# A decoder block on one core: forget gates computed in the first value projection, a third gate tile ahead of the recurrent projections, the causal mask added by VectorE, norm steps reordered

## The reference, cut to what matters

```python
xr = causal_dwconv(xr, w_rnn_conv[l], b_rnn_conv[l])
hr = rg_lru(xr, w_lru_a[l], b_lru_a[l], w_lru_i[l], b_lru_i[l], lru_lambda[l])
y_rnn = gelu(gr) * hr
log_f = log_sigmoid(fl + b_fgate[l])
F = cumsum(log_f, axis=1)                                    # over the tokens, by head
s = q k^T / sqrt(128) + F[q] - F[k], masked to k <= q        # by head, in blocks of 128 tokens
y_attn = softmax(s) v
merged = g_r * (y_rnn @ w_proj_rnn) + g_a * (y_attn @ w_proj_attn)
x = x + gate1 * (merged @ w_out)
h = modulate(rmsnorm(x, g_norm2), shift2, scale2)            # then the ConvFFN, and a last modulated norm
```

## Time and profile before

| | |
|---|---|
| median of 3 runs (lowest, highest) | 983.5 us (982.2, 983.51) |
| the profiled execution: time, span | 983.65 us, 981.9 us |
| TensorE (PE) busy | 968.5 us, 99% |
| VectorE (DVE) busy | 635.5 us, 65% |
| ScalarE (ACT) busy | 415.8 us, 42% |
| mean granted TensorE clock | 0.993 |
| waits of TensorE on the trace | 3.1, 1.2, 1.0, 0.7 and 0.5 us, one each |
| DMA | 129.37 MB, mean 132 GB/s |

### The profile page before, as it was taken

How to read it: one execution, slowest core, us unless ns; L and a number is a source line. 1 busy time by engine, 2 the same in 40 slices (tenths; PEclk the granted TensorE clock), 3 DMA queues, 4 the chain that set the end, 5 groups by cost and what they waited for, 6 DMA issues and landing times.

```text
span 981.9 us, 12554 instructions
## 1 busy us (share of the span) xinstructions
PE 968.5 (99%) x4739; PEld 816.5 (83%) x4739; DVE 635.5 (65%) x856; ACT 415.8 (42%) x548; POOL 2.2 (0%) x12
## 2 busy tenths in 40 slices
PE   8999999999999999999999999999999999999997
PEld 8878887788888888989888889888888888888875
DVE  3789998522668797853758555777674344754665
ACT  6479777322426354352623373322232222422331
POOL 0000000000000000000000000000000000000000
PEclk9899999999999999999999999999999999999999
DMA  9743311334674435432217505666532332233201
GB/s 326 249 139 102 102 43 49 96 96 131 210 232 151 153 116 181 129 107 86 86 44 259 192 21 172 196 200 202 180 118 86 105 109 85 86 106 136 100 20 67
DMA packets 105775, 129.37 MB, mean 132 GB/s; under 512 B 4636, under 2 KB 81156, under 8 KB 105612
## 3 DMA queue, kind: packets, MB, share of 16 engines
q1 hardware_dynamic: 105192, 126.75, 39.5%
q10 hardware_dynamic: 548, 2.14, 0.6%
HBM read 126.77 MB, written 2.11 MB: 131 GB/s over the span
## 4 chain that ended last, share of the span: by engine, by line
PE 94%; DVE 3%; DMA 1%; SPq 1%; issue 0%; ACT 0%; DVEq 0%; ACTq 0%
PE ps L1667 30%; PE ps L1669 30%; PE ps L1668 30%; DMA ada_first<-in_w_ada 1%; PE ps L1900 1%; PE ps L1711 1%; DVE wsplit_x L1570 0%; DVE wraw_x L1566 0%; PE ps L1726 0%; PE ps L1719 0%; PE ps L1701 0%; PE ps L1700 0%; PE ps L2017 0%; DVE act_s L1583 0%; SPq L447 0%
## 5 line engine op out<-in xcount | busy, mean ns | idle before, releaser
L1667 PE MATMUL ps<-h,wsplit 128*128 128x512 f32 (+1 forms) x816 | 312.7, 383 | 1.2 <-DVE h L1539 1.2
L1669 PE MATMUL ps<-h,wsplit 128*128 128x512 f32 (+1 forms) x816 | 310.9, 381 | 0.0
L1668 PE MATMUL ps<-h,wsplit 128*128 128x512 f32 (+1 forms) x816 | 310.8, 381 | 0.0
L988 DVE TENSOR_TENSOR wsplit<-wraw,wsplit 128x2048 fp32r<-128x2048 f32 (+2 forms) x79 | 167.0, 2114 | 101.6 <-ACT wsplit L596 64.1
L1667 PEld LDWEIGHTS ps<-h,wsplit 128*128 128x128 f32 x816 | 153.6, 188 | 29.9 <-issue 1.4
L1669 PEld LDWEIGHTS ps<-h,wsplit 128*128 128x128 f32 x816 | 153.4, 188 | 29.5
L1668 PEld LDWEIGHTS ps<-h,wsplit 128*128 128x128 f32 x816 | 153.5, 188 | 28.8
L596 ACT ACTIVATE wsplit<-wraw 128x2048 fp32r<-128x2048 f32 (+2 forms) x69 | 120.9, 1752 | 105.2 <-PE ps L1669 104.8
L1596 DVE SCALAR_TENSOR_TENSOR cv<-ps,vec,cv 128x511 f32<-128x511 f32 (+1 forms) x48 | 35.9, 748 | 55.7 <-ACT cv L945 52.6
L1041 DVE SCALAR_TENSOR_TENSOR ada_acc<-ada_raw,small,ada_acc 128x512 f32<-128x512 f32 x84 | 63.1, 751 | 2.7
L1667 PE MATMUL ps<-wsplit,act_s 128*128 128x512 f32 x160 | 62.3, 390 | 0.7 <-DVE act_s L1583 0.7
(11 more groups left out here) (248 smaller groups left out, 1415.7 us busy)
## 6 DMA issues: line engine op xcount, KB each, us to landing
wraw<-in_w_ffn_up SPq DMA_DIRECT2D x24, 1024.0 KB, 5.1
wraw<-in_w_in SPq DMA_DIRECT2D x23, 1024.0 KB, 5.3
ada_raw<-in_w_ada SPq DMA_DIRECT2D x16, 1024.0 KB, 6.7
wraw<-in_w_ffn_down SPq DMA_DIRECT2D x10, 1024.0 KB, 4.9
ada_first<-in_w_ada SPq DMA_DIRECT2D x8, 1024.0 KB, 12.1
ada_raw<-in_w_ada_final SPq DMA_DIRECT2D x8, 1024.0 KB, 5.1
wraw<-in_w_in SPq DMA_DIRECT2D x12, 512.0 KB, 3.8
wraw<-in_w_proj_rnn SPq DMA_DIRECT2D x8, 640.0 KB, 4.4
```

Of the source, the lines that this page charges most:

```text
L988: ve.tensor_tensor(wsplit[:, s, LO, 0:n], wraw[:, s, 0:n], wsplit[:, s, HI, 0:n].bitcast(F), ALU.subtract).then_inc(w_lo, 1)
L1667: te.matmul(dst, lhs(LO), rhs(HI), start=start, stop=False)
L1668: te.matmul(dst, lhs(HI), rhs(LO), start=False, stop=False)
L1669: return te.matmul(dst, lhs(HI), rhs(HI), start=False, stop=stop)
```

## The change

- The forget-gate product and its small weight buffer go. The first value projection (`v_first`) is made ahead of q and k, with weights `vw` of 256 + 8 columns, into four banks; its last eight columns are the forget gates, tokens on partitions. Their log-sigmoid is computed there, four transposes bring it to 8 partitions for the scan, and the transposes for `nFq` move between the two k tiles. The chunk order becomes v, q, k; the q tiles of pair 0 use banks 5 and 6. SP stores and reloads `nF` inside the first `load_step`.
- The third gate tile is made where the forget-gate product was, in bank 3. The loop of pairs has five rounds instead of six, and projections 13, 14 and 15 follow each other.
- No mask matmul: VectorE makes `nFm`, F plus the mask on each diagonal block, once for each head, and each `scores_add` is split in the part below the diagonal block and the block.
- `lam_rest` is cut: six steps stay before `h_low(4)`, seven go behind `xr_split(0, 1)`. `keep_clock(6, 1)` is put ahead of the second group of vector transposes.
- `h2_low(b - 2)` stands between the halves of `x1_block(b)`. Mean and root of the second and the last norm take the first half's sum earlier, and the Newton step is one instruction shorter behind the root.

The diff, cut (indentation shortened by eight):

```diff
+nFm = [at("nFm0", 192, [P, NB, P]), at("nFm1", 198, [P, NB, P])]
...
+maskf = at("maskf", 201, [P, P])
...
+vw = [at("vw_hi", 160, [P, KD, 256 + H], F32R), at("vw_lo", 178, [P, KD, 256 + H], F32R)]
+fl1 = at("fl1", 203.5, [P, NB, H])
+fl2 = at("fl2", 203.75, [P, NB, H])
...
+def qk_bank(i, which, t):
+    return 5 + t if which == 0 and isinstance(i, int) and i == 0 else t
...
+    load(C_MIX + 2, 0, cols_of(w_in_v, COL_MR + 2 * P, P), KD, P)
+    with sp.Fori(0, KD - 3) as j:
+        load(C_MIX + 3, j, cols_of(w_pr_v, P * j, P), NR, P)
+        load(C_MIX + 4, j, cols_of(w_in_v, COL_MR + 3 * P + P * j, P), KD, P)
+    load(C_MIX + 13, 0, cols_of(w_pr_v, 5 * P, P), NR, P)
...
+    load(C_ATT, 0, cols_of(w_in_v, COL_V, 256), KD, 256)
+    load(C_ATT + 1, 0, cols_of(w_in_v, COL_Q, 256), KD, 256)
+    load(C_ATT + 2, 0, cols_of(w_in_v, COL_K, 256), KD, 256)
...
+        if i4 == 4:
+            sp.wait_ge(fl_step, 7)
+            sp.dma_start(nF_dram, nF[:, :]).then_inc(nF_stored, 16)
+            sp.wait_ge(nF_stored, 16)
+            load_nF(0)
         load(C_ATT, i4, cols_of(w_in_v, COL_Q + 64 * i4, 256), KD, 256, 1)
         load(C_ATT + 1, i4, cols_of(w_in_v, COL_K + 64 * i4, 256), KD, 256, 1)
...
     gates_exp(i, 0)
+    hi(C_MIX + 2, 0, KD * P)
     gates_exp(i, 1)
-    hi(C_MIX + 2, 0, NR * P)
-    gates_sqrt(i)
+    ae.wait_ge(q_done, 2 * i + 1)
+    ae.activation(ev[:, 0], ev[:, 0], ACT.Sqrt).then_inc(sqrt_done, 1)
+    hi(C_MIX + 3, 0, NR * P)
+    ae.wait_ge(q_done, 2 * i + 2)
+    ae.activation(ev[:, 1], ev[:, 1], ACT.Sqrt).then_inc(sqrt_done, 1)
...
     hi(C_ATT + 1)
+    v_first_hi(0)
+    v_first_hi(1)
+    ae.wait_ge(fl_step, 3)
+    ae.activation(fl2[:, :, :], fl2[:, :, :], ACT.Exp).then_inc(fl_act, 1)
+    ae.wait_ge(fl_step, 4)
+    ae.activation(fl2[:, :, :], fl2[:, :, :], ACT.Ln).then_inc(fl_act, 1)
+    hi(C_ATT + 2)
     qk_hi(0, 0, 0)
     qk_hi(0, 1, 0)
-    hi(C_ATT + 2)
+    hi(C_ATT + 3)
     qk_hi(0, 0, 1)
     qk_hi(0, 1, 1)
-    hi(C_ATT + 3)
-    v_hi(0, 0)
-    v_hi(0, 1)
...
+    def mean_block(m, ss, b, summed, mean):
+        ve.wait_ge(summed, 2 * b + 1)
+        ve.tensor_scalar(m[:, b:b + 1], ss[:, 2 * b:2 * b + 1], 1.0 / D, EPS, ALU.mult, ALU.add)\
+          .then_inc(mean, 1)
+        ve.wait_ge(summed, 2 * b + 2)
+        ve.wait_ge(mean, 2 * b + 1)
+        ve.scalar_tensor_tensor(m[:, b:b + 1], ss[:, 2 * b + 1:2 * b + 2], 1.0 / D, m[:, b:b + 1],
+                                ALU.mult, ALU.add).then_inc(mean, 1)
+    def rsqrt_block(r, m, b, mean, rooted, done):
+        ve.wait_ge(mean, 2 * b + 2)
+        mh = mhalf[:, b:b + 1]
+        ve.tensor_scalar(mh, m[:, b:b + 1], -0.5, None, ALU.mult).then_inc(half_done, 1)
+        ve.wait_ge(rooted, b + 1)
+        rb = r[:, b:b + 1]
+        ve.reciprocal(rb, rb).then_inc(done, 1)
+        ve.wait_ge(done, 3 * b + 1)
+        t = newton_t[:, 0:1]
+        ve.scalar_tensor_tensor(t, rb, mh, rb, ALU.mult, ALU.mult).then_inc(done, 1)
+        ve.wait_ge(done, 3 * b + 2)
+        ve.scalar_tensor_tensor(rb, t, 1.5, rb, ALU.add, ALU.mult).then_inc(done, 1)
+        ve.wait_ge(done, 3 * b + 3)
     newton_n = 0
     def newton(r, m):
 @ -1136,9 +1187,12 @@
         for d in (13, 11, 9):
             lam_times(d)
...
+    def lam_next():
...
     def lam_rest():
-        for d in (7, 5, 3, 1):
-            lam_times(d)
+        lam_times(1)
...
-    lam_rest()
+    lam_next()
...
-    ve.wait_ge(fw_hi, 1)
-    ve.tensor_tensor(fws[:, LO].rearrange("p k h -> p (k h)"), fw[:, :, :].rearrange("p k h -> p (k h)"),
-                     fws[:, HI].rearrange("p k h -> p (k h)").bitcast(F), ALU.subtract).then_inc(fw_lo, 1)
+    lam_rest()
...
+    lo(C_MIX + 2, 0, KD * P)
     decay(i, (1,))
     recur(i, 0)
+    lo(C_MIX + 3, 0, NR * P)
...
+        ve.tensor_tensor(merged_a[:, j], ps[:, bank, :], merged_a[:, j], ALU.mult).then_inc(mixa_done, 1)
+    with ve.Fori(0, KD - 3) as j:
+        lo(C_MIX + 4, j, KD * P)
+        gate_product(j, C_MIX + 3, 2, j)
+        lo(C_MIX + 5, j, NR * P)
+    lo(C_MIX + 14, 0, NR * P)
+    gate_product(KD - 3, C_MIX + 13)
     lo(C_MIX + 15, 0, NR * P)
...
     gate_product(KD - 2, C_MIX + 14)
-    lo(C_ATT)
-    gate_product(KD - 1, C_MIX + 15)
-    ve.wait_ge(nFq_mm, 1)
-    ve.tensor_copy(nFq[:, :, :].rearrange("p b h -> p (b h)"), ps[:, 3, 0:NB * H]).then_inc(fl_step, 1)
-    ve.wait_ge(fl_step, 7)
+    ve.wait_ge(w_hi, C_ATT + 1)
+    ve.tensor_tensor(vw[LO][:, :, 0:256], wraw[:, C_ATT % 2].rearrange("p (k n) -> p k n", k=KD),
+                     vw[HI][:, :, 0:256].bitcast(F), ALU.subtract).then_inc(w_lo, 1)
+    ve.wait_ge(fw_hi, 1)
+    ve.tensor_tensor(vw[LO][:, :, 256:256 + H], fw[:, :, :], vw[HI][:, :, 256:256 + H].bitcast(F),
+                     ALU.subtract).then_inc(fw_lo, 1)
+    gate_product(KD - 1, C_MIX + 15, 1)
...
         if t == 0:
             ve.wait_ge(nF_loaded, 16 * i)
+        ve.tensor_tensor(nFm[t][:, :, :], nFb[:, t].rearrange("p (b k) -> p b k", b=NB),
+                         maskf[:, :].rearrange("p (b k) -> p b k", b=1).broadcast_to([P, NB, P]),
+                         ALU.add).then_inc(nf_masked, 1)
...
+            nfq = nFq[:, qb, ds(2 * (i - 1) + t, 1)]
             ve.wait_ge(s_mm, 8 * (i - 1) + 4 * t + S_READY[turn])
-            ve.scalar_tensor_tensor(pr, ps[:, bank, a:a + n], nFq[:, qb, ds(2 * (i - 1) + t, 1)],
-                                    nFb[:, t, 0:n], ALU.subtract, ALU.add).then_inc(s_add, 1)
+            if qb:
+                ve.scalar_tensor_tensor(pr[:, 0:n - P], ps[:, bank, a:a + n - P], nfq, nFb[:, t, 0:n - P],
+                                        ALU.subtract, ALU.add).then_inc(s_below, 1)
+            if turn == 0:
+                ve.wait_ge(nf_masked, 2 * (i - 1) + t + 1)
+            ve.scalar_tensor_tensor(pr[:, n - P:n], ps[:, bank, a + n - P:a + n], nfq, nFm[t][:, qb],
+                                    ALU.subtract, ALU.add).then_inc(s_add, 1)
             ve.wait_ge(s_add, 8 * (i - 1) + 4 * t + turn + 1)
+            if qb:
+                ve.wait_ge(s_below, 6 * (i - 1) + 3 * t + turn)
             ve.tensor_reduce(nmx[:, t, qb:qb + 1], pr, AX_X, ALU.max, negate=True).then_inc(s_max, 1)
...
     lo(C_ATT + 1)
     ada2(4, 0, 4)
+    v_first_lo(0)
+    ada2(4, 4, 7)
+    v_first_lo(1)
+    ve.wait_ge(fl_step, 2)
+    ve.scalar_tensor_tensor(fl2[:, :, :], fl1[:, :, :], -1.0, fl1[:, :, :], ALU.mult, ALU.min)\
+      .then_inc(fl_step, 1)
+    ada2(4, 7, 8)
+    ve.wait_ge(fl_act, 1)
+    ve.tensor_scalar(fl2[:, :, :], fl2[:, :, :], 1.0, None, ALU.add).then_inc(fl_step, 1)
+    ve.tensor_scalar(fl1[:, :, :], fl1[:, :, :], 0.0, None, ALU.min).then_inc(fl_step, 1)
+    ada2_halves(4)
+    ve.wait_ge(fl_act, 2)
+    ve.wait_ge(fl_step, 5)
+    ve.tensor_tensor(fl1[:, :, :], fl2[:, :, :], fl1[:, :, :], ALU.subtract).then_inc(fl_step, 1)
+    lo(C_ATT + 2)
     qk_lo(0, 0, 0)
+    ada2(5, 0, 3)
     qk_lo(0, 1, 0)
-    lo(C_ATT + 2)
-    ada2(4, 4, 7)
+    ve.wait_ge(fl_mm, 1)
+    ve.wait_ge(consts, 6)
+    ve.tensor_tensor_scan(nF[:, :], onesrow[:, :], ps[0:H, 3, :], 0.0, ALU.mult, ALU.add)\
+      .then_inc(fl_step, 1)
+    lo(C_ATT + 3)
     qk_lo(0, 0, 1)
-    ada2(4, 7, 8)
-    ada2_halves(4)
-    ada2(5, 0, 3)
-    qk_lo(0, 1, 1)
-    lo(C_ATT + 3)
+    ve.wait_ge(nFq_mm, 1)
+    ve.tensor_copy(nFq[:, :, :].rearrange("p b h -> p (b h)"), ps[:, 2, 0:NB * H]).then_inc(fl_step, 1)
+    ve.wait_ge(fl_step, 8)
+    ada2(5, 3, 8)
     ve.wait_ge(g1_loaded, 16)
     gate1_store(4, 0)
-    v_lo(0, 0)
-    ada2(5, 3, 8)
     ada2_halves(5)
-    v_lo(0, 1)
+    qk_lo(0, 1, 1)
...
-    def x1_block(b):
+    def x1_block(b, between=None):
         for half in range(2):
+            if half and between:
+                between()
             n, cs = 2 * b + half, slice(T * half, T * half + T)
...
+        mean_block(ms2, ss2, b, ms2_sum, ms2_mean)
+        rsqrt_block(rs2, ms2, b, ms2_mean, ms2_sqrt, rs2_done)
...
-        x1_block(b)
-        if b > 1:
-            h2_low(b - 2)
+        x1_block(b, (lambda: h2_low(b - 2)) if b > 1 else None)
...
+        mean_block(ms3, ss3, b, ms3_sum, ms3_mean)
+        rsqrt_block(rs3, ms3, b, ms3_mean, ms3_sqrt, rs3_done)
...
     ada_first_total(0, 0)
+    keep_clock(6, 1)
...
-    proj_rnn(C_MIX + 2, 2, 0, lambda k: te.wait_ge(y_part, 2 * k + 2))
-    te.wait_ge(sigr_done, 2)
-    gate_mr(C_MIX + 3, 0)
-    with te.Fori(1, KD - 2) as j:
+    gate_mr(C_MIX + 2, 3)
+    proj_rnn(C_MIX + 3, 2, 0, lambda k: te.wait_ge(y_part, 2 * k + 2))
+    te.wait_ge(sigr_done, 1)
+    gate_mr(C_MIX + 4, 0)
+    with te.Fori(1, KD - 3) as j:
         te.wait_ge(mixa_done, j)
-        proj_rnn(C_MIX + 2, 2, j)
-        te.wait_ge(sigr_done, j + 2)
-        gate_mr(C_MIX + 3, 0, j)
+        proj_rnn(C_MIX + 3, 2, j)
+        te.wait_ge(sigr_done, j + 3)
+        gate_mr(C_MIX + 4, 0, j)
+    te.wait_ge(mixa_done, KD - 3)
+    proj_rnn(C_MIX + 13, 2)
     te.wait_ge(mixa_done, KD - 2)
     proj_rnn(C_MIX + 14, 2)
```

(37 more changed lines are left out.)

154 lines of the change are left out of this document (56 added, 98 removed).

## The result

The changed kernel takes 973.3 us in the median of four runs (972.5 to 975.9) against 983.5: the ratio is 0.991, with a 95% interval of 0.9898 to 0.9923. The forecast was 972.0, with 970 to 976 around it. The profiled execution took 974.08 (span 972.3), so the profiles stand 9.6 us apart where the sum had 11.7.

The account below looks back on a forecast made before the run. TensorE was taken as the bound, busy 968.5 of 981.9 us. Against 983.65 the terms -5.53 + 0.33 + 0.50 - 4.1 + 1.15 - 1.0 - 1.85 - 0.85 - 0.35 = -11.7 gave 972.0 us, range 970 to 976.

Parts of the forecast that it names:

- Removed forget gates and the new stall: Recurrent projections: 24 matmuls go, minus 5.53 us; TensorE newly waits for bank 2 before C_MIX+14, plus 1.15 (0.9 to 1.3).
- 264 columns: First value projection: 96 matmuls grow from 256 to 264 columns, plus 0.33 us (0 to 0.5).
- Transposes: Four transposes added for gates that come out with tokens on partitions: plus 0.50 us.
- The mask on TensorE: Score groups: 32 bf16 mask matmuls go, minus 4.1 us, or 3.4 without the delay of the matmul behind.
- VectorE's cover: Pairs of heads: VectorE's added 2.2 to 3.5 us a pair fits in 4.8 of slack, so costs nothing.
- tight covers miss: Rival: mask delay partly stays, third gate tile or first pair wait 1 us or so together; 973.7 to 975, chance 0.12.
- The clock: Start: new keep_clock calls delay the clock's fall, and it is back before the projections; minus 1.85 us, best case minus 2.2.
- The rival (the calls only cost 0.9): Start: the clock falls anyway, so plus 0.9 replaces minus 1.85; 974.8 us, chance 0.2.
- Lambda: Start: seven of VectorE's lambda steps move behind xr_split(0,1), so TensorE's stall before h_low(4) goes; minus 1.0 us.
- Second norm: h_low(1) between the halves of x1 shortens TensorE's wait before 577.32; minus 0.85 us (0.4 to 1.2).
- Tail: Last norm: two of VectorE's small steps leave the path, one partly hidden; minus 0.35 us.
- Third gate tile, queues: Reordered loads cost nothing; the third gate tile's split is the tightest cover, 0 to 0.5 us.

Follow-up runs that it names:

- e_bank3: The changed kernel with the projection of C_MIX+14 in bank 3 instead of bank 2; median 972.33 us, ratio 0.99 to the kernel before.
- e_dve_more: The changed kernel with the 512-column masked row computed twice in each of the 8 score steps; median 977.79 us, ratio 0.9948 to the kernel before.
- e_mask_te: The changed kernel with the causal mask back on TensorE as 32 bf16 matmuls; median 976.24 us, ratio 0.9934 to the kernel before.
- e_nfm_early: The changed kernel with the masked row of t=0 made one pair ahead on VectorE; median 972.46 us, ratio 0.9894 to the kernel before.

## Why the prediction was right, and where it was not

**Removed forget gates and the new stall: right.** -5.53 + 1.15 against -4.38 measured; e_bank3 puts 1.12 on the stall alone.

**264 columns: mis-sized.** 0.09 for 0.33. Eight columns cost 0.001 us each time, not 0.0034: the slope between 256 and 512 columns doesn't show so near 256 in this trace.

**Transposes: about right**, 22.83 against 22.24 for the Q and K work with them: 0.59 for 0.50.

**The mask on TensorE: nearly right.** 0.95 a pair, 3.8 in all, for 4.1; the matmul behind the scores of a head keeps 0.01 and the scores 0.04 of the delay.

**VectorE's cover: the step that failed.** The added work was sized well (1.47 a step, 1.17 in the last two pairs). The text set it and the 1.1 of later start against 4.8 us of slack, up to the weighted sum. That sum counted the 0.67 of idle time before the reciprocal, which is no slack: VectorE waits there for the exponential that its own last maximum released, and it is there after the change too, at 309.24. And it left out that a faster TensorE wants pt 0.95 earlier. What was left is 4.8 - 0.67 - 0.95 = 3.2. The first pair needs 2.9 + 1.1 = 4.0: 0.8 short, 0.90 lost.

The text also had only the last of two places where TensorE waits for VectorE. The other comes first: the last two transposes need the scores of t=1 read. Before the change VectorE had read them at 310.16 and TensorE came for the bank near 313.9, so the cover there was 3.8, with the 0.56 of idle time at 306.61 4.3, and less the 0.95 again 3.4 against the same 4.0. Of the 0.8 us, 0.53 are lost here (308.28 instead of 307.75) and 0.28 at the weighted sum.

The second pair needs 2 x 1.47 = 2.9 of the 3.2 and has 0.3 to spare; e_dve_more, which adds 1.6, makes it 1.43 longer. The third needs 2.3 and loses 0.39 of that 1.6. The last pair loses 0.27: the work ahead of its weighted sum is only 18 matmuls long, where the others have 24. e_mask_te and e_nfm_early show that all this is VectorE's share of the mask, and that 0.68 us less of it is enough. This is the part of the rival "tight covers miss" that names the first pair, come on top of the main case; the third gate tile did not wait.

**The clock: mis-sized, mechanism half right.** -1.85 forecast; -0.74 in the pair of profiles, and 0 to 0.7 for the calls over the runs. Two parts of that step failed. The clock was not back before the projections, so the time won at full clock was given back in h matmuls at half. And the start has a bound close by: with the clock up all the time, TensorE waits 0.80 for h. The rival (the calls only cost 0.9) did not come either. It drew on the Trainium skill (TensorE: Matmul & The Clock Gate, "HAM oscillation"), where a fall follows long idle gaps; the traces speak against that here, since in the changed kernel TensorE was busy for all of 18 to 25 us and the clock fell behind it.

**Lambda: right**, -0.92 for -1.0. **Second norm: mis-sized**, -1.25 for -0.85: the wait of 1.20 went entirely, and the 0.3 set aside for a later ScalarE did not show. **Tail:** -0.27 for -0.35, by the landmarks alone. **Third gate tile, queues: right**, nothing (the stage up to 173.94 is even 0.09 shorter).

So the time was met from a sum 2 us too good: the profiled start fell 1.2 us short of the forecast and the cover 1.2, the norm gave 0.4 more, and the median run started some 0.8 earlier than the profiled one. That last part is luck: the start is a draw, and nothing in the forecast foresaw it. The range had its wide side where the misses lay.

## What to carry to other kernels

Count as slack of an engine only idle time that ends with another engine's independent work; a wait for the answer to its own last step travels with it. Do the sum for every place where the bound engine waits for that engine, not only for the last one. When the bound engine gets faster, subtract what it gains from every cover beside it. And if a kernel's start varies from run to run, compare from the first landmark behind it: there the profiles of this one repeat to 0.1 us, where the whole time differs by 2 us and more.

## What the runs showed of the hardware that I had not expected

- TensorE's clock at the start is a draw. The same code ran at the half level (1.2 GHz) from 25.5 to 32.3 us in one execution and not at all in another. Of the 14 profiles two show no fall, the others one between 21.4 and 27.0 us, and one of them a second at 31.6. The two profiled executions of the changed kernel differ by 1.3 us at the start; they are 0.12 apart before the fall (23.32 and 23.20, the same one-column matmuls).
- 264 columns cost nearly the same as 256: 0.1208 against 0.1199 us a matmul, over 96.
- A wait that goes can give back more than its idle time: the stall printed as 0.85 was worth 1.12. The next start came 1.01 late (242.96 for 241.95), since idle time is counted only from the modelled end of the matmul before, and the matmul behind the wait started its own successor 0.11 late (0.34 instead of 0.23).
- The pause of VectorE between a row and its maximum was 0.13 us in the first two pairs and 0.03 in the last two, for the same instructions.
